# Splitting the first weight panels before a join, and moving modulation panels, in a four-layer hybrid backbone on one core

## The chip, the cores and the metric

One core of a Trainium2 chip runs the whole program. The metric is the device time of one execution in microseconds; the time of a kernel is the median of its runs. The kernel before was run three times: 2142.14 us in the median, 2142.07 to 2143.4 us. TensorE is called PE in the profile, VectorE DVE, ScalarE ACT, GpSimd POOL, and SyncE SP.

## The reference, cut to what matters

```
for i in range(4):                       # mixers: attention, Hyena, S5, FNet
    mod_l = split(silu(c) @ mod_w[i] + mod_b[i], 6)      # the same for ctx with silu(c_ctx)
    hl = modulate(rmsnorm(xl, mix_pre_g[i]), mod_l[0], mod_l[1])
    yl = mixer_i(hl, hc)
    xl = xl + mod_l[2] * rmsnorm(yl, mix_post_g[i])
    hl = modulate(rmsnorm(xl, ffn_pre_g[i]), mod_l[3], mod_l[4])
    xl = xl + mod_l[5] * rmsnorm(swiglu(hl, ffn_w13[i], ffn_w2[i]), ffn_post_g[i])
```

All is float32. There are 256 latent and 256 context tokens, the model is 1024 wide and the SwiGLU 2816. The context is carried through layers 0 and 1 (512 tokens a stage), read by layer 2, and not needed by layer 3, so the later stages work on 256 tokens.

## The kernel before, in words

**Layout.** Activations are held transposed: 8 slices (k or c, 0 to 7) of 128 channels on the partitions, 512 or 256 tokens along the free axis. A float32 product is made of three products of rounded halves: `product` (L930 to L935) multiplies w_hi by h_hi, w_hi by h_lo and w_lo by h_hi. So each weight panel (1024 x 256, 1 MB) goes through `Split` (L840 to L911): it lands in `ring`, which has two slots; ACT rounds it in two halves into w_hi (`round`, L887); DVE subtracts, also in two halves, into w_lo (`remain`, L894). w_hi and w_lo hold two panels each. A slot of the ring is loaded again once its panel is split; SP issues those loads in one fixed order (`sp_issue`, L202).

**Joins.** Between a mixer and its SwiGLU, and between a SwiGLU and the next mixer, stands a `Join` (L530 to L753); there are eight, called here by layer as mid 0, post 0, mid 1, ..., post 3. While the stage before gives its last products, `move` (ACT, L567) and `cross` (DVE, L596) take each slice c: its square, its gain, and the products for the next norm's sum. Then come `root_post` (L643), a reciprocal (L708), five small DVE operations (L713 to L721), `root_pre` (L648) and a second reciprocal (L732). Each of the two results is spread over the partitions by PE (L481), first r_post into bank 5, then r_pre into bank 4. Then, slice by slice, DVE runs scaled (L690), update (L695) and normed (L700), ACT applies the modulation (L673) and rounds (L677), and DVE makes h_lo (L704, `remainder`). Those last two exist where the next stage takes split activations (`parts`): all four mid joins and post 0. There PE starts with `lead_in` (L913): as slice k becomes ready, it does the 12 products of that slice with the first two weight panels; after half of the slices it releases the slot for half of the third panel (`stepped`).

**Panels split around a join.** Where `early` is set (layer 0), the first panel's halves are rounded at c = 5 of `move`; elsewhere ACT rounds them around root_pre. All remainders of the first two panels are on DVE inside `Join.vector`: panel 0 half 0 before scaled(0), then panel 1 half 0 after slice 0, and the other two halves after slices 2 and 3. The first half of panel 2 is rounded after slice 5.

**Modulation panels.** The 24 vectors of mod_l (units) are computed from 96 weight panels of 1 MB, four a unit, each in 8 matmuls of 32 columns that show as 16 rows (L402, bank 7, MODB). `mods.place` gives panels to places in the program in a fixed order; where a place begins after a unit is complete, PE first transposes that unit (`turn`, L377, into bank 6). ACT copies MODB to mod_rows (L413) once the unit's fourth panel is done; DVE reads the transpose in `mods.vector` (L423 to L434). `turn` waits for ACT's copy of its own unit and, by `wait_read`, for DVE's reading of the unit turned before it:

```
def wait_read(self, pe):
    if self.turned_by_pe:
        pe.wait_ge(mod_ready, self.ready0[self.turned_by_pe - 1] + 1)
```

Panels lie in a ring of two (mod_ring). `mods.refill(sp, upto)` (L357) issues the next loads in SP's order, each behind a wait for the use of the panel whose slot it takes.

**Places before.** Layer 0's SwiGLU has 16 panels, behind every other step; mid 0, post 0 and mid 1 have (2, 2): two before the first spread, two behind the second. Post 1 has (2, 0); mid 2, post 2 and mid 3 have (2,). The S5 mixer has 4 ("states"), 2 ("scan") and 2 ("turns").

**The S5 mixer** (L2386 to L2820). PE injects 16 batches of groups and transposes them (L2688, L2707), then multiplies by a Toeplitz matrix (L2725). Meanwhile DVE scans, with POOL for half the groups. ACT copies the states of the first half (`forward`, L2757), and PE multiplies them by the output weights (L2738, first half: 128 matmuls), runs the two "scan" panels, and after ACT's second `forward` the second half. ACT copies the unit of the scan panels before its second forward. DVE reads all modulation units of this mixer only after its scan is finished (`backward`, then `mods.vector`). SP loads, in this order: injection weights, two mod panels, the Toeplitz matrix, output weights of the first half, those of the second half once L2725 is done, mod panels, and, after the scan, the panels of the gated unit (`self.up`, w_glu). In the gated unit ACT makes a sigmoid (L2802), DVE the gated value (L2593), and ACT calls `post.move` (mid 2) one chunk later.

## Time and profile before

| what | value |
|---|---|
| median of three runs | 2142.14 us |
| the profiled execution's own time | 2140.99 us |
| its span | 2139.2 us |
| PE busy (matmul) | 2023.3 us, 95% |
| PE busy (weight load) | 1623.0 us, 76% |
| DVE busy | 1230.4 us, 58% |
| ACT busy | 887.1 us, 41% |
| POOL busy | 166.5 us, 8% |
| DMA | 342.18 MB, mean 160 GB/s |
| granted PE clock, mean | 0.98 |

The busy times are over the whole span; the program is a chain of stages, so an engine that is half idle overall can still be the one that others wait for in a join. The profile's own times start with the span; about 1.8 us of the execution lie around it.

### The profile page before, as it was taken

To read this page: it belongs to the slowest core of one execution; us is meant where nothing else is said; L and a number is where in the kernel's file an instruction comes from. 1 tells how busy PE (TensorE), PEld (TensorE's weight loads), DVE (VectorE), ACT (ScalarE), POOL (GpSimd) and SP (SyncE) were. 2 spreads that over 40 slices of the span, in tenths; PEclk is the share of its full clock that TensorE was granted. 3 is DMA by queue.
4 is the path that set the end of the run, shared out by engine and by line. 5 is a ranking of instruction groups with operands and counts; after the bars stand their busy time and mean duration, and the time that the engine had idled before them with its cause. 6 is when DMAs were issued, how large, how long until landed. Compare 5 with 4: busy or idle time off the path is not lost.

```text
span 2139.2 us, 32361 instructions
## 1 busy us (share of the span) xinstructions
PE 2023.3 (95%) x13489; PEld 1623.0 (76%) x13489; DVE 1230.4 (58%) x2056; ACT 887.1 (41%) x1464; POOL 166.5 (8%) x255
## 2 busy tenths in 40 slices
PE   6999999999999999999999999998658999999998
PEld 4765566777777767767768888876357999789997
DVE  5233553556566557668564665764975645656454
ACT  3432334443333353323553344235645544545444
POOL 0000100102101101001010210020320000000000
PEclk9999999999999999999999999999879999999999
DMA  8434341545435546443243433343984555425552
GB/s 307 160 115 175 132 158 61 166 143 181 173 121 171 195 164 230 158 157 113 94 145 102 133 123 121 121 150 126 334 296 158 178 184 184 157 80 163 185 184 99
DMA packets 227246, 342.18 MB, mean 160 GB/s; under 512 B 9590, under 2 KB 190625, under 8 KB 224860
## 3 DMA queue, kind: packets, MB, share of 16 engines
q1 hardware_dynamic: 216064, 310.27, 42.1%
q0 software_dynamic: 10320, 29.58, 4.7%
q8 instruction: 107, 1.75, 0.3%
q10 hardware_dynamic: 716, 0.26, 0.0%
q14 instruction: 39, 0.32, 0.0%
HBM read 317.66 MB, written 24.51 MB: 160 GB/s over the span
## 4 chain that ended last, share of the span: by engine, by line
PE 85%; DVE 7%; DMA 3%; ACT 2%; POOL 1%; issue 1%; SPq 0%; ACTq 0%; DVEq 0%; POOLq 0%
PE bank L933 24%; PE bank L934 23%; PE bank L935 23%; PE bank L402 3%; PE bank L1417 1%; DMA arena<-mod_w 1%; PE bank L622 1%; PE bank L1848 1%; PE bank L2212 1%; PE bank L612 1%; DMA mod_ring<-mod_w 1%; DMA ring<-s_w_glu 1%; PE bank L2090 1%; PE bank L1391 1%; PE bank L1807 1%
## 5 line engine op out<-in xcount | busy, mean ns | idle before, releaser
L933 PE MATMUL bank<-h_hi,w_hi 128*128 128x512 f32 (+1 forms) x1480 | 511.7, 346 | 11.9 <-DVE h_lo L704 8.1
L934 PE MATMUL bank<-h_lo,w_hi 128*128 128x512 f32 (+1 forms) x1480 | 504.1, 341 | 0.0
L935 PE MATMUL bank<-h_hi,w_lo 128*128 128x512 f32 (+1 forms) x1480 | 504.0, 341 | 0.0
L894 DVE TENSOR_TENSOR w_lo<-ring,w_hi 128x1024 fp32r<-128x1024 f32 (+1 forms) x282 | 323.9, 1185 | 288.1 <-ACT w_hi L887 288.0
L933 PEld LDWEIGHTS bank<-h_hi,w_hi 128*128 128x128 f32 x1480 | 282.6, 191 | 50.4 <-DVE h_lo L704 10.6
L887 ACT ACTIVATE w_hi<-ring 128x1024 fp32r<-128x1024 f32 (+1 forms) x282 | 274.2, 1019 | 104.8 <-PE bank L935 102.5
L935 PEld LDWEIGHTS bank<-h_hi,w_lo 128*128 128x128 f32 x1480 | 282.6, 191 | 32.0 <-issue 0.2
L934 PEld LDWEIGHTS bank<-h_lo,w_hi 128*128 128x128 f32 x1480 | 283.1, 191 | 29.3 <-issue 0.2
L933 PE MATMUL bank<-g_hi,w_hi 128*128 128x512 f32 (+1 forms) x704 | 241.1, 342 | 0.0
L934 PE MATMUL bank<-g_lo,w_hi 128*128 128x512 f32 (+1 forms) x704 | 236.9, 337 | 0.0
L935 PE MATMUL bank<-g_hi,w_lo 128*128 128x512 f32 (+1 forms) x704 | 236.7, 336 | 0.0
L933 PEld LDWEIGHTS bank<-g_hi,w_hi 128*128 128x128 f32 x704 | 133.5, 190 | 22.7 <-issue 8.7
L935 PEld LDWEIGHTS bank<-g_hi,w_lo 128*128 128x128 f32 x704 | 133.6, 190 | 14.2
L934 PEld LDWEIGHTS bank<-g_lo,w_hi 128*128 128x128 f32 x704 | 133.6, 190 | 12.9
L1136 ACT ACTIVATE g_hi<-arena 128x512 fp32r<-128x512 f32 (+1 forms) x88 | 45.9, 525 | 234.5 <-DVE arena L1161 234.5
L1130 ACT ACTIVATE arena<-bank 128x512 f32<-128x512 f32 (+1 forms) x88 | 42.7, 490 | 190.4 <-PE bank L935 188.7
L402 PE MATMUL bank<-mod_ring,silu_c 128*32 128x256 f32 x1408 | 95.4, 394 | 23.1 <-DMA mod_ring<-mod_w 23.1
L1161 DVE TENSOR_TENSOR arena<-arena,bank 128x512 f32<-128x512 f32 (+1 forms) x88 | 48.2, 551 | 111.8 <-PE bank L935 110.5
L402 PEld LDWEIGHTS bank<-mod_ring,silu_c 128*32 128x32 f32 x1408 | 40.4, 111 | 61.5 <-DMA mod_ring<-mod_w 26.7
L933 PE MATMUL bank<-h_hi,hy_w_hi 128*128 128x512 f32 x192 | 76.6, 399 | 0.0
L934 PE MATMUL bank<-h_lo,hy_w_hi 128*128 128x512 f32 x192 | 75.3, 392 | 0.0
L935 PE MATMUL bank<-h_hi,hy_w_lo 128*128 128x512 f32 x192 | 75.0, 391 | 0.0
(391 smaller groups left out, 3179.3 us busy)
## 6 DMA issues: line engine op xcount, KB each, us to landing
ring<-ffn_w SPq DMA_DIRECT2D x120, 1024.0 KB, 5.1
mod_ring<-mod_w SPq DMA_DIRECT2D x88, 1024.0 KB, 6.9
ring<-ffn_w SPq DMA_DIRECT2D x16, 768.0 KB, 4.6
ring<-hy_w_in SPq DMA_DIRECT2D x12, 1024.0 KB, 5.2
arena<-mod_w SPq DMA_DIRECT2D x8, 1024.0 KB, 17.0
s_in_weights<-arena POOLq DMA_DIRECT2D x32, 256.0 KB, 3.0
s_out_weights<-arena POOLq DMA_DIRECT2D x16, 512.0 KB, 3.4
arena<-s_in_weights SPq DMA_DIRECT2D x8, 1024.0 KB, 7.1
```

Of the source, the lines that this page charges most:

```text
L402: last = nc.tensor.matmul(MODB[32 * g:32 * g + 32, 0:256], silu_c[:, k, :], self.slot(m)[:, kk, 256 * g:256 * g + 256], start=(k == 0), st ...
L612: last = nc.tensor.matmul(bank[5][32 * g:32 * g + 32, 0:P], ones[:, :], SQ[:, c, g * P:(g + 1) * P], start=(c == 0), stop=(c == KD - 1))
L622: last = nc.tensor.matmul(bank[4][32 * g:32 * g + 32, 0:2 * P], ones[:, :], self.zx[:, c % 2, g, :, :].rearrange("p z t -> p (z t)"), star ...
L887: nc.scalar.activation(self.hi[:, i % SPLIT, a:b], self.w.slot(i)[:, a:b], ACT.Copy).then_inc(w_rounded, 1)
L894: last = unit.tensor_tensor(self.lo[:, i % SPLIT, c:c + w], self.w.slot(i)[:, c:c + w], self.hi[:, i % SPLIT, c:c + w].bitcast(F32), ALU.s ...
L933: nc.tensor.matmul(o, w[0], v[0], start=first, stop=False)
L934: nc.tensor.matmul(o, w[0], v[1], start=False, stop=False)
L935: return nc.tensor.matmul(o, w[1], v[0], start=False, stop=last)
L1130: nc.scalar.activation(self.silus[:, q, 0:n], self.out(i, q)[:, 0:n], ACT.Silu).then_inc(ffn_silu, 1)
L1136: nc.scalar.activation(g_hi[:, c + q, 0:n], self.silus[:, q, 0:n], ACT.Copy).then_inc(ffn_g_rounded, 1)
L1161: nc.vector.tensor_tensor(self.silus[:, q, 0:n], self.silus[:, q, 0:n], self.out(i, q)[:, 0:n], ALU.mult).then_inc(ffn_product, 1)
L1391: nc.tensor.matmul(b[:, :], self.qn[:, hd, q], self.kn[:, hd, :], start=True, stop=False)
```

## The change

The first two weight panels behind each join with `first` are rounded inside `move` (c = 4, 5, 6; all four halves at c = 4 for mid 2). For the mid joins DVE makes their remainders inside `cross` (c = 5 and 6; for mid 2 in the S5 mixer's loop at c = 5); post 0 keeps DVE's old order. The third panel's first half is rounded behind all slices. The first spread comes before the modulation panels, and each spread is followed by one panel (post 2, mid 2 and mid 3 had two before the first). The four panels so freed in layer 0 and two of mid 1's go elsewhere: layer 0's SwiGLU takes 20 instead of 16, and the S5 mixer 10 instead of 8: two ("turned") behind the injections, two ("states") and two ("late") behind the Toeplitz product, then "scan" and "turns" as before. Refills stand in front of the output weights of each half. Buffers of the S5 and FNet mixers are moved out of the way of w_hi and w_lo.

```diff
@@ class Join
+            ROUNDS = {4: ((0, 0), (0, 1)), 5: ((1, 0),), 6: ((1, 1),)}
+            REMAINDERS = {5: ((0, 0), (1, 0)), 6: ((0, 1), (1, 1))}
...
@@ Join.move
-                if self.early and c == KD - 3:
-                    self.first.round(act, 0, 0)
-                    self.first.round(act, 0, 1)
+                if self.first:
+                    for panel, half in self.rounds.get(c, ()):
+                        self.first.round(act, panel, half)
@@ Join.cross
+                if self.first:
+                    for panel, half in self.remainders.get(c, ()):
+                        self.first.remain(dve, panel, half)
@@ Join.tensor
+                pe.wait_ge(*self.small.after(1))
+                spread(bank[5], r_post, self.n).then_inc(j_spread, 1)
                 if self.fills:
                     mods.tensor(pe, (self, 0))
-                pe.wait_ge(*self.small.after(1))
-                spread(bank[5], r_post, self.n).then_inc(j_spread, 1)
@@ Join.scalar
-                if self.first and not self.early:
-                    self.first.round(act, 0, 0)
                 self.root_pre(act)
-                if self.first:
-                    if not self.early:
-                        self.first.round(act, 0, 1)
-                    self.first.round(act, 1, 0)
-                    if self.parts:
-                        self.first.round(act, 1, 1)
...
-                        if k == 5:
-                            self.first.round(act, 2, 0)
+                if self.first:
+                    self.first.round(act, 2, 0)
@@ Join.vector
-                if self.first:
+                if self.first and not self.remainders:
                     self.first.remain(dve, 0, 0)
...
-                        if k == 0:
-                            self.first.remain(dve, 1, 0)
-                        if k in (2, 3):
-                            self.first.remain(dve, k - 2, 1)
+                        if not self.remainders:
+                            if k == 0:
+                                self.first.remain(dve, 1, 0)
+                            if k in (2, 3):
+                                self.first.remain(dve, k - 2, 1)
@@ class S5
+            ROUNDS = {4: ((0, 0), (0, 1), (1, 0), (1, 1))}
+            REMAINDERS = {"gates": 5}
...
-                mods.place((self, "states"), 4, p0 + 0.4)
+                mods.place((self, "turned"), 2, p0 + 0.3)
+                mods.place((self, "states"), 2, p0 + 0.35)
+                mods.place((self, "late"), 2, p0 + 0.4)
                 mods.place((self, "scan"), 2, p0 + 0.4)
@@ S5.sync
                 for c in range(8):
                     toeplitz(c)
+                mods.refill(sp, p0 + 0.3)
                 sp.wait_ge(self.e_summed, self.injected(self.NB - 1))
                 for hf in range(2):
                     if hf:
                         sp.wait_ge(self.m_summed, 1)
+                        mods.refill(sp, p0 + 0.35)
@@ S5.vector
                 self.backward(dve, V.tensor_copy, 1, self.moved_dve)
-                for key in ("states", "scan"):
+                for key in ("turned", "states", "late", "scan"):
                     mods.vector(dve, (self, key))
...
+                    if c == self.REMAINDERS["gates"]:
+                        for half in range(2):
+                            for panel in range(2):
+                                self.post.first.remain(dve, panel, half)
@@ S5.tensor
+                mods.tensor(pe, (self, "turned"))
                 pe.wait_ge(self.m_loaded, 16 * (1 + 8))
...
-                mods.tensor(pe, (self, "states"))
+                for key in ("states", "late"):
+                    mods.tensor(pe, (self, key))
@@ S5.scalar
-                mods.scalar(act, (self, "states"))
+                for key in ("turned", "states", "late"):
+                    mods.scalar(act, (self, key))
@@ stages
-        TICKS = {0: lambda i: i % 2 if i < 32 else 0, 1: lambda i: 0, 2: lambda i: 0, 3: lambda i: 0}
+        TICKS = {0: lambda i: int(i % 3 > 0 and i < 30), 1: lambda i: 0, 2: lambda i: 0, 3: lambda i: 0}
...
             if l < 2:
-                mid.place_mods()
+                mid.place_mods((1, 1))
             else:
-                mid.place_mods((2,))
+                mid.place_mods((1, 1))
             ffn = Ffn(l, n_out, mid, post, TICKS[l])
             if l == 0:
-                post.place_mods()
+                post.place_mods((1, 1))
             if l == 1:
-                post.place_mods((2, 0), (len(panels) + 0.2, None))
+                post.place_mods((1, 1), (len(panels) + 0.2,) * 2)
             if l == 2:
-                post.place_mods((2,))
+                post.place_mods((1, 1))
```

## Rows read from the trace of the kernel before

**Rows 1.** The page's groups: ACT's rounding of half a panel (busy, mean ns | idle)

```profile
L887 ACT ACTIVATE w_hi<-ring 128x1024 fp32r<-128x1024 f32 (+1 forms) x282 | 274.2, 1019 | 104.8 <-PE bank L935 102.5
```

**Rows 2.** Timeline of mid 0: start, duration, engine, line, operation, [idle before <- releaser]

```profile
362.37 1.91 PE L402 MATMUL bank<-mod_ring,silu_c 128*32 128x256 f32 x32
...
364.06 1.22 DVE L894 TENSOR_TENSOR w_lo<-ring,w_hi 128x1024 fp32r<-128x1024 f32 x1
...
365.40 0.69 DVE L690 TENSOR_TENSOR arena<-arena,bank 128x512 f32<-128x512 f32 x1
...
370.78 0.69 DVE L704 TENSOR_TENSOR h_lo<-arena,h_hi 128x512 fp32r<-128x512 f32 x1
...
371.22 1.07 PE L402 MATMUL bank<-mod_ring,silu_c 128*32 128x256 f32 x16 [1.41 <-DMA mod_ring<-mod_w]
...
384.53 0.50 PE L933 MATMUL bank<-h_hi,w_hi 128*128 128x512 f32 x1 [0.52 <-DVE h_lo L704]
...
395.55 0.38 PE L377 MATMUL bank<-ident,mod_rows 128*128 128x128 f32 x2
```

**Rows 3.** Timeline of mid 1

```profile
1087.10 0.69 DVE L690 TENSOR_TENSOR arena<-arena,bank 128x512 f32<-128x512 f32 x1 [0.52 <-PE bank L481]
...
1092.47 0.69 DVE L704 TENSOR_TENSOR h_lo<-arena,h_hi 128x512 fp32r<-128x512 f32 x1
...
1117.46 0.38 PE L377 MATMUL bank<-ident,mod_rows 128*128 128x128 f32 x2
```

**Rows 4.** Timeline of post 0

```profile
804.77 0.69 DVE L704 TENSOR_TENSOR h_lo<-arena,h_hi 128x512 fp32r<-128x512 f32 x1
...
816.71 0.38 PE L377 MATMUL bank<-ident,mod_rows 128*128 128x128 f32 x2
```

**Rows 5.** Timeline of PE in mid 2 and mid 3 (256 tokens)

```profile
1656.06 0.48 PE L933 MATMUL bank<-h_hi,w_hi 128*128 128x256 f32 x1 [2.11 <-DVE h_lo L704]
...
1671.75 0.38 PE L377 MATMUL bank<-ident,mod_rows 128*128 128x128 f32 x2
...
1927.66 0.58 PE L933 MATMUL bank<-h_hi,w_hi 128*128 128x256 f32 x1 [2.11 <-DVE h_lo L704]
...
1940.35 0.39 PE L933 MATMUL bank<-h_hi,w_hi 128*128 128x256 f32 x1 [0.81 <-DVE h_lo L704]
...
1943.33 0.38 PE L377 MATMUL bank<-ident,mod_rows 128*128 128x128 f32 x2
```

**Rows 6.** Timeline of DVE in post 1 and post 2: the first use of bank 5

```profile
1490.35 0.69 DVE L690 TENSOR_TENSOR arena<-arena,bank 128x512 f32<-128x512 f32 x1 [1.26 <-PE bank L481]
...
1861.93 0.42 DVE L690 TENSOR_TENSOR arena<-arena,bank 128x256 f32<-128x256 f32 x1 [0.82 <-PE bank L481]
```

**Rows 7.** The chain in order of time: a modulation panel, a weight panel's load

```profile
395.93 1.00 PE bank L402 x16
...
1660.97 5.21 DMA ring<-ffn_w
```

**Rows 8.** End of the S5 mixer: SP's loads and ACT's sigmoid

```profile
1628.50 8.47 SPq L213 DMA_DIRECT2D ring<-ffn_w  x2
...
1641.03 0.47 ACT L2802 ACTIVATE arena<-bank,vec 128x256 f32<-128x256 f32 x1 [6.68 <-PE bank L935]
```

**Rows 9.** Timeline of the S5 mixer around the end of the scan

```profile
1563.27 1.94 PE L402 MATMUL bank<-mod_ring,silu_c 128*32 128x256 f32 x16 [15.24 <-DMA mod_ring<-mod_w]
...
1570.31 5.37 PE L2738 MATMUL bank<-arena,tail 128*32 128x128 f32 x128 [2.70 <-ACT tail L2757]
...
1576.73 0.17 DVE L423 TENSOR_TENSOR modv<-bank,vec 128x16 f32<-128x16 f32 x1
...
1577.92 2.82 SPq L213 DMA_DIRECT2D ring<-s_w_glu  x2
```

**Rows 10.** Windows in that mixer: length, busy of five engines, PEclk, DMA share, GB/s

```profile
1555.00:1560.00 5.00, 0.00 (x0) 0.00 (x0) 4.69 (x13) 0.00 (x0) 4.84 (x3) 0.50 1.00 414
```

**Rows 11.** DMA issues from 1540 to 1550 us: times, KB, median us to landing

```profile
mod_ring<-mod_w SPq DMA_DIRECT2D x2, 1024.0 KB, 17.0
```

More of the change, by code:

```diff
@@ L530, in build, with __init__ @@
         class Join:
-            def __init__(self, n, post, pre, scratch, parts=False, split=False, early=False):
+            ROUNDS = {4: ((0, 0), (0, 1)), 5: ((1, 0),), 6: ((1, 1),)}
+            REMAINDERS = {5: ((0, 0), (1, 0)), 6: ((0, 1), (1, 1))}
+            def __init__(self, n, post, pre, scratch, parts=False, split=False, rounds=ROUNDS, remainders=REMAINDERS):
                 self.n, self.post, self.pre, self.zx = n, post, pre, scratch
-                self.parts, self.split, self.early = parts, split, early
+                self.parts, self.split = parts, split
+                self.rounds, self.remainders = rounds, remainders
                 self.rows = n // 4
@@ L2461, in __init__ @@
                 p0 = len(panels)
-                mods.place((self, "states"), 4, p0 + 0.4)
+                mods.place((self, "turned"), 2, p0 + 0.3)
+                mods.place((self, "states"), 2, p0 + 0.35)
+                mods.place((self, "late"), 2, p0 + 0.4)
                 mods.place((self, "scan"), 2, p0 + 0.4)
                 mods.place((self, "turns"), 2, p0 + RING)
-                self.y_hi, self.y_lo = (place(n, KD * TOK + a, [KD, LAT], F32R) for n, a in (("s5_y_hi", 10240), ("s5_y_lo", 8192)))
+                self.y_hi, self.y_lo = (place(n, KD * TOK + a, [KD, LAT], F32R) for n, a in (("s5_y_hi", 24576), ("s5_y_lo", 26624)))
                 self.y_rounded, self.y_split = Tally(mix_rounded, KD), Tally(mix_split, KD)
-                hi, lo = (place(n, KD * TOK + 12288 + i * SPLIT * KD * 256, [SPLIT, KD * 256], F32R) for i, n in enumerate(("s5_w_hi", "s5_w_lo")))
+                slots = place("s5_w", KD * TOK + 16384, [SPLIT, 2, KD * 256], F32R)
+                hi, lo = slots[:, :, 0], slots[:, :, 1]
                 self.up = Gated("s5_glu", A["s5_w_glu"][0], D, lambda k: (self.y_hi[:, k, :], self.y_lo[:, k, :]), LAT,
@@ L2824, in __init__ @@
                 self.f_hi = place("fn_f_hi", KD * TOK + 26624, [KD, LAT], F32R)
-                self.f_lo = place("fn_f_lo", KD * TOK + 13568, [KD, LAT], F32R)
+                self.f_lo = place("fn_f_lo", 3 * P * KD * 8 + KD * TOK, [KD, LAT], F32R)
                 hi, lo = (place(n, KD * TOK + 16384 + i * SPLIT * KD * 256, [SPLIT, KD * 256], F32R) for i, n in enumerate(("fn_w_hi", "fn_w_lo")))
@@ L2913, in build @@
                 joins.append(Opening(stages[0], mod))
-            joins.append(Join(spans[l][1], (mod, 1), (mod, 2), scratch["arena" if l == 0 else "tail"], parts=True, early=(l == 0)))
+            joins.append(Join(spans[l][1], (mod, 1), (mod, 2), scratch["arena" if l == 0 else "tail"], parts=True,
+                              rounds=S5.ROUNDS if l == 2 else Join.ROUNDS, remainders=S5.REMAINDERS if l == 2 else Join.REMAINDERS))
             nxt = [m for m in live if m > l]
             pre = (Modulation(nxt[0]), 0) if nxt else None
-            joins.append(Join(spans[l][1], (mod, 3), pre, scratch["tail"], parts=(l == 0), split=(l == 1), early=(l == 0)))
+            joins.append(Join(spans[l][1], (mod, 3), pre, scratch["tail"], parts=(l == 0), split=(l == 1), remainders={}))
         stages.append(joins[0])
```

## The prediction

> **What bounds the kernel.** I read the page first. PE is busy for 95% of the span (the table above), so a step of PE that is moved costs time unless it falls into one of PE's gaps. The chain of waits, in order of time, shows where those gaps are: at the joins, at the end of the S5 mixer's scan, and at some loads. So I went through each join and through that mixer in the timeline, engine by engine.
>
> In mid 0 the reader should see three things. Two modulation panels hold PE for 1.91 us, from 362.37, in front of the first spread. Bank 5 is first used at 365.40. Slice 0 of h_lo is complete at 371.47, but PE still waits for a modulation load (371.22) and does that panel before it starts the lead-in. From slice 4 on (384.53) the lead-in runs without a wait to 395.55: 11.02 us for 4 slices, 2.755 a slice [rows 2].
>
> **Lead-ins of 512 tokens.** The change takes four remainders of 1.2 us [rows 2] out of DVE's sequence in the mid joins and puts the spread in front of the panels. In mid 0 the small operations end when the first remainder begins, at about 364.1 (the durations of neighbours overlap a little); scaled(0) starts at 364.15 instead of at 365.40, and the second reciprocal, the second spread and slice 0 follow 1.25 us earlier: h_lo(0) at 370.2. DVE then has four operations of at most 0.69 us a slice, no more than PE's 2.755, so PE runs through: 370.25 + 8 x 2.755 = 392.3 instead of 395.55 [rows 2]. **Mid 0: -3.25.** The rounding moved into `move` lies beside the mixer's last products: PE takes 2 x 2.755 us for an output slice, and ACT rounds half a panel in 1.02 us [rows 1], at most two a slice. Were that cover gone, four halves would cost 4.1. Of the panels behind the spreads, one each is loaded before the join, so none waits there.
>
> Mid 1 has the same shape. There scaled(0) waited 0.52 for the spread behind a remainder; without both it starts at 1085.45 instead of 1087.10, so h_lo(0) ends at 1093.16 - 1.65 = 1091.5, and the lead-in at 1113.55 instead of 1117.46 [rows 3]. **-3.9.**
>
> Post 0 keeps DVE's order. Only PE's panels get out of the way, and slice 4, complete at 805.46, still sets the end: 805.46 + 11.02 = 816.5 against 816.71 [rows 4]. **-0.2**, though two panels fewer stand there.
>
> **Lead-ins of 256 tokens.** Mid 3 starts at 1927.66 and ends at 1943.33; its last two slices take 2.98 us [rows 5] with a slow first product, so 1.45 a slice. The remainder taken out in front of scaled(0) brings 0.9 (the root then ends last, not the remainder). End: 1926.76 + 8 x 1.45 = 1938.35. **Mid 3: -5.0.** Mid 2 starts at 1656.06 and ends at 1671.75 [rows 5]; in the same way 1655.16 + 11.6 = 1666.75, **-5.0**. The third panel's load, which used to wait for the split of the first, starts before its need in both.
>
> Mid 2 pays for it in front. All four roundings stand behind slice 4 there. SwiGLU panel 1 is issued last of the two loads, at 1628.50 + 8.47 - 0.37 = 1636.6 [rows 8]; a free load takes 5.2 [rows 7], so it lands at 1641.8. ACT stands behind that wait in its order, then has two roundings of 1.02 [rows 1]: until 1643.9. The sigmoid of chunk 6, which started at 1641.03 [rows 8], is queued behind it; DVE's three remaining remainders run until 1646.3, 4.8 us after it used to take chunk 6. About 1.6 us of idle time between that and `move` absorb a part. **+3.2**, between 2.8 and 4.8.
>
> **Joins without early panels.** In post 1 and post 2 DVE waited 1.26 and 0.82 us for bank 5, behind the panels [rows 6]. The first becomes **-1.25**; of the second the root leaves **-0.7**.
>
> **Layer 0's SwiGLU** gets four more panels. Each costs PE its 1.00 us [rows 7], as PE has no gap there: **+4.0**.
>
> **The S5 mixer** is where the change has a wait of its own. Before, unit 19 was transposed and read in layer 1's SwiGLU, so `turn` of unit 20 had nothing to wait for at the "states" panels. Now the shifted count completes unit 19 in post 1; it is transposed in "turned", and DVE reads it only after the scan, at 1576.73 [rows 9]. The "late" place begins with `turn(20)`, whose `wait_read` asks for just that reading. PE stands there, and behind it stand the late panels and the first half's output product, which started at 1570.31. From DVE's 1576.9: transpose 0.4, two late panels 2 x 1.9 (at the duration of 1563.27), output product 5.4, two scan panels 1.9 [rows 9, 2], and 0.5 for SP: 1588.9. Their use lets SP go on to the gated unit's weights, issued at 1577.92 before: +11.0. ACT's second `forward` hangs on the scan panels too. The scan panels' own loads are issued behind the late panels at 1579.3 and 1581.1; with 5.2 each [rows 7] they land by 1586.5, as the output product ends.
>
> How fast PE is there is open. Around the scan's end PE idles, and its granted clock is 0.50 of full speed, the 1.2 GHz level [rows 10]; one panel took 1.94 us there against 0.95 in the joins [rows 9, 2]. At full clock throughout, late panels cost 1.9 and the product perhaps half of 5.4, and only the loads (1584.8 for the second) hold the rest: +8.9. I take **+10.5**, nearer to the slow end, as those rows stand in the same place after the same idling.
>
> The Trainium skill ("TensorE: Matmul & The Clock Gate", section "What's actually happening") says that an idle array is throttled by default and only activity releases it. By that rule alone the late panels would be slow and the sum 0.5 us higher; the rows agree at 0.50 with PE idle. It speaks against the change: the refilled gap lies behind the longest idling.
>
> The "turned" and "states" panels lie in PE's wait for the Toeplitz load and behind that product; without the hold they would be hidden. The two loads that go in front of each half's output weights delay these by some 5 us each, long before their use.
>
> **Sum.** -3.25 - 3.9 - 0.2 - 5.0 - 5.0 + 3.2 - 1.25 - 0.7 + 4.0 + 10.5 = -1.6. Against the profiled execution's 2140.99 that is 2139.4; the median lies 1.15 above that execution, so 2140.5. A measurement of this kernel can tell about 0.2% (4.3 us) from no change.
>
> **Rivals.** (a) *PE isn't held in the S5 mixer*: if DVE's reading comes earlier than I read the order, the late panels hide as before, and 10.5 goes: 2130.0. For it: before, PE idled 15.24 us there at no cost [rows 9]. Against it: one semaphore, one order of DVE's program. 12%.
>
> (b) *Slower*: the loads behind the hold are late. The scan panels' loads can only start once the late panels are used, and the gated unit's weights follow them in SP's order. In this mixer mod loads took 17.0 us to land when output weights stood in front of them [rows 11]. At that, the second lands at 1598.1, the scan panels end at 1599.1, and SP follows at 1599.6: +21.7 instead of +10.5, 2151.7. It decides from a landing of about 6 us on; it makes the whole kernel measurably slower from about 12. Against it: the output weights, issued at some 1550, are gone when the hold ends, and the queue is empty. 8%.
>
> (c) *The lead-ins still stop*: DVE's and ACT's operations, or the third panel's load, pace them rather than PE. Two stops of 0.5 us, like those of 0.52 and 0.81 now [rows 2, 5], in each of the four mid lead-ins make 4.0: 2144.5. For it: DVE's four operations are as long as PE's share of a slice. Against it: the durations overlap, and the 1.2-us remainders were what broke the pace. 12%.
>
> **Numbers.** The forecast has 68%; its own bounds (+8.9 to +11.5 for the hold, 2.8 to 4.8 in mid 2, half a microsecond for each join) give 2137 to 2144. Rival (a) lies below, (c) at the upper edge. The range 2133 to 2146 leaves out (a)'s centre, (b) and little else. Faster by over 0.2% needs 2137.9 or less: (a) with 12%, and 14% from the forecast's lower edge, 26%. Slower by over 0.2% needs 2146.4: (b), and a little of (c), 10%. The rest, 64%, is no change.
>
> **What would show it.** Each mid join's lead-in without a wait for h_lo, 22.0 us long at 512 and 11.6 at 256 tokens; bank 5's first use without a wait for PE; ACT waiting for a ring load behind slice 4 in the S5 mixer's end. Above all PE's L377 in the S5 mixer released by DVE's L423, 30 us after the states panels, the output product some 11 us after ACT's first forward, and the next load of w_glu that much later. The prediction falls if L402 ("late") is released by its load around 1560 and the output product follows ACT directly, or if the lead-ins still stop at slices 3 and 4.

## The result and the profile after

The changed kernel takes 2147.51 us (median of 14 runs, 2146.01 to 2148.59) against 2142.16 (14 runs of the kernel before beside it): a ratio of 1.0024, 95% interval 1.0016 to 1.0031. It is slower by 5.4 us, where 2140.5 was forecast with a range up to 2146. The profiled execution took 2146.01 us with a span of 2144.2, 5.0 more than the span before.

The page's head, after: PE is busy for as long as before (2022.7 us against 2023.3), so the 5 us are waiting, not work.

```profile
span 2144.2 us, 32362 instructions
PE 2022.7 (94%) x13489; PEld 1617.9 (75%) x13489; DVE 1230.0 (57%) x2056; ACT 887.9 (41%) x1464; POOL 166.5 (8%) x255
PEclk9999999999999999999999999999879999999998
```

Where they arise is read best from one instruction that stands at the same place of every join: ACT's root of the output norm (L643 before, L652 after, two or three lines lower in some experiments). The table has its first start and then the time from each join's root to the next one's, all from the timeline of ACT. The experiments of the next section are in it too. Each row is one profiled execution, which lies up to 3.5 us from the median of its kernel (e8), so medians and rows need not differ by the same amount.

| kernel | mid 0 at | to post 0 | to mid 1 | to post 1 | to mid 2 | to post 2 | to mid 3 | to post 3 | span |
|---|---|---|---|---|---|---|---|---|---|
| before | 360.97 | 421.00 | 300.15 | 403.80 | 162.00 | 210.26 | 61.36 | 207.70 | 2139.2 |
| after | 360.43 | 421.92 | 300.81 | 400.83 | 176.66 | 207.73 | 60.66 | 202.72 | 2144.2 |
| e1 | 361.50 | 423.56 | 301.08 | 399.48 | 164.09 | 206.61 | 62.26 | 202.74 | 2133.3 |
| e2 | 361.02 | 421.97 | 299.96 | 401.07 | 177.89 | 207.74 | 60.67 | 202.75 | 2145.5 |
| e3 | 361.90 | 423.50 | 299.72 | 401.05 | 169.36 | 211.03 | 60.67 | 204.21 | 2143.4 |
| e4 | 361.33 | 421.23 | 301.69 | 405.46 | 163.92 | 207.20 | 60.99 | 203.28 | 2137.1 |
| e5 | 360.69 | 421.93 | 300.50 | 401.06 | 161.80 | 206.91 | 60.67 | 203.28 | 2128.8 |
| e6 | 360.79 | 421.94 | 300.26 | 401.04 | 164.47 | 207.29 | 60.85 | 202.74 | 2131.3 |
| e7 | 361.18 | 421.38 | 298.66 | 401.14 | 173.89 | 207.35 | 60.77 | 202.75 | 2139.1 |
| e8 | 360.80 | 419.96 | 298.88 | 401.33 | 167.54 | 207.41 | 60.71 | 202.73 | 2131.3 |
| e9 | 360.65 | 421.93 | 300.59 | 401.08 | 162.09 | 206.74 | 62.28 | 203.99 | 2131.3 |
| e10 | 360.48 | 421.93 | 300.60 | 400.98 | 161.35 | 211.08 | 62.28 | 205.37 | 2136.0 |
| e11 | 360.65 | 425.23 | 300.55 | 402.73 | 162.61 | 207.32 | 60.86 | 202.74 | 2134.6 |

One column stands out: the stretch with post 1 and the S5 mixer became 14.66 us longer. All others together became 10.1 us shorter up to the last root (the earlier start of mid 0, 0.5, is in this), and 0.5 was lost behind it.

**The S5 mixer.** PE's timeline of the changed kernel around the scan (start, duration, engine, line, operation, idle time before it and releaser); it answers to [rows 9]:

```profile
1529.22 0.38 PE L377 MATMUL bank<-ident,mod_rows 128*128 128x128 f32 x2
...
1537.41 6.22 PE L2740 MATMUL bank<-arena 128*32 128x128 f32 x128 [5.94 <-DMA arena<-s_toeplitz]
1543.45 1.90 PE L402 MATMUL bank<-mod_ring,silu_c 128*32 128x256 f32 x32
1573.30 0.66 PE L377 MATMUL bank<-ident,mod_rows 128*128 128x128 f32 x2 [27.95 <-DVE modv L423]
1573.88 3.32 PE L402 MATMUL bank<-mod_ring,silu_c 128*32 128x256 f32 x32
1577.03 3.67 PE L2754 MATMUL bank<-arena,tail 128*32 128x128 f32 x128
1580.99 1.07 PE L402 MATMUL bank<-mod_ring,silu_c 128*32 128x256 f32 x16 [0.29 <-DMA mod_ring<-mod_w]
1584.97 1.07 PE L402 MATMUL bank<-mod_ring,silu_c 128*32 128x256 f32 x16 [2.91 <-DMA mod_ring<-mod_w]
```

Unit 19 is transposed at 1529.22 and read by DVE at 1572.97; `turn(20)` in front of the late panels waits 27.95 us for that reading, as forecast. The first output product stands behind it. ACT's `forward` and `backward` (L2773) ran from 1562.38 for 4.03 us, so the product could have started at about 1566.5; it started at 1577.03. Then comes a second wait, of 2.91 us, for the load of the second scan panel. SP's own timeline gives the end of the chain, again against [rows 9]:

```profile
1575.88 10.59 SPq L363 DMA_DIRECT2D mod_ring<-mod_w  x4
1586.57 1.04 SPq L213 DMA_DIRECT2D ring<-s_w_glu  x2
```

The gated unit's weights are issued at 1586.57 instead of 1577.92. DVE's reading came 3.76 us earlier than before (1572.97 against 1576.73), so from that reading on the loss is 8.65 + 3.76 = 12.4 us.

**The joins.** PE in mid 0 and post 0, after, against [rows 2] and [rows 4]:

```profile
365.11 1.16 PE L481 MATMUL bank<-r_pre,sel 128*128 128x128 f32 x8 [1.02 <-DVE r_pre L733]
366.20 1.07 PE L402 MATMUL bank<-mod_ring,silu_c 128*32 128x256 f32 x16
369.63 0.50 PE L935 MATMUL bank<-h_hi,w_hi 128*128 128x512 f32 x1 [2.35 <-DVE h_lo L705]
...
391.61 1.07 PE L402 MATMUL bank<-mod_ring,silu_c 128*32 128x256 f32 x16
...
788.17 2.01 PE L481 MATMUL bank<-r_pre,sel 128*128 128x128 f32 x8 [2.15 <-DVE r_pre L733]
790.12 1.81 PE L402 MATMUL bank<-mod_ring,silu_c 128*32 128x256 f32 x16
793.54 0.50 PE L935 MATMUL bank<-h_hi,hy_w_hi 128*128 128x512 f32 x1 [1.61 <-DVE h_lo L705]
```

In mid 0 the lead-in runs from 369.63 to 391.61 without a stop, 21.98 us for the 22.04 forecast. In post 0 the spread takes 2.01 instead of 1.16 us: PE has idled for 2.15 us behind its single panel and works more slowly. The same in mid 2, where PE comes out of the mixer's end, with the windows of that stretch (length; busy PE, PEld, DVE, ACT, POOL; PEclk; DMA share; GB/s):

```profile
1662.38 1.22 PE L481 MATMUL bank<-r_post,sel 64*128 64x128 f32 x4
1663.53 1.93 PE L402 MATMUL bank<-mod_ring,silu_c 128*32 128x256 f32 x16
1665.45 1.22 PE L481 MATMUL bank<-r_pre,sel 64*128 64x128 f32 x4
1666.59 1.93 PE L402 MATMUL bank<-mod_ring,silu_c 128*32 128x256 f32 x16
1668.78 0.58 PE L935 MATMUL bank<-h_hi,w_hi 128*128 128x256 f32 x1 [0.25 <-DVE h_lo L705]
```

```profile
1656.00:1660.00 4.00, 1.82 (x14) 0.67 (x16) 2.34 (x10) 3.11 (x7) 0.00 (x0) 0.83 0.00 0
1660.00:1664.00 4.00, 3.23 (x20) 1.51 (x24) 2.74 (x8) 0.98 (x3) 0.00 (x0) 0.50 0.00 0
...
1668.00:1672.00 4.00, 3.75 (x23) 3.22 (x16) 3.82 (x13) 3.08 (x7) 0.00 (x0) 0.50 1.01 354
1672.00:1676.00 4.00, 4.00 (x34) 4.00 (x34) 3.97 (x13) 3.06 (x7) 0.00 (x0) 0.96 1.04 370
```

PE's clock stands at its lower level, 0.50, from the first spread to the first 3 us of the lead-in. Mid 3 of the same execution has the same code and the same 256 tokens, and there PE is at full speed; its lead-in starts 7.22 us behind the root (8.13 in mid 2) and ends 18.83 us behind it (21.28):

```profile
1930.43 0.71 PE L481 MATMUL bank<-r_post,sel 64*128 64x128 f32 x4
1933.43 0.71 PE L481 MATMUL bank<-r_pre,sel 64*128 64x128 f32 x4 [1.29 <-DVE r_pre L733]
...
1936.26 0.39 PE L935 MATMUL bank<-h_hi,w_hi 128*128 128x256 f32 x1 [1.11 <-DVE h_lo L705]
```

### The profile page after: what moved, and what is told of

The parts are those of the page before. It is cut to its first block, busy times and chain, and to the rows that moved or that the text cites. A ratio compares the mean times of both kernels' runs of the same rounds, so it can differ in the third digit from the quotient of the medians.

```text
span 2144.2 us, 32362 instructions
## 1 busy us (share of the span) xinstructions
PE 2022.7 (94%) x13489; PEld 1617.9 (75%) x13489; DVE 1230.0 (57%) x2056; ACT 887.9 (41%) x1464; POOL 166.5 (8%) x255
## 4 chain that ended last, share of the span: by engine, by line
PE 86%; DVE 7%; DMA 2%; ACT 2%; POOL 1%; issue 1%; SPq 1%; ACTq 0%; DVEq 0%; POOLq 0%
PE bank L935 24%; PE bank L936 23%; PE bank L937 23%; PE bank L402 3%; PE bank L1419 1%; PE bank L1850 1%; PE bank L2214 1%; PE bank L631 1%; DMA ring<-mla_w_in 1%; DMA mod_ring<-mod_w 1%; PE bank L621 1%; PE bank L2092 1%; DVE arena L701 1%; PE bank L1393 1%; PE bank L1809 1%
```

## Experiments

Theory H: DVE's late reading of unit 19 holds PE, and that is the S5 mixer's loss. Rival R1: the two extra loads and the refills in front of the output weights. Rival R2: the moved splits bring nothing. For the mid 2 join there were three more theories: B, that ACT's wait for a load costs time (e5); C, that the late load of the third panel does (e6); K, that PE comes to the join slow and the panels there don't matter (e10). Edits are against the changed kernel unless said.

### e1: DVE reads unit 19 between the halves of the scan

```diff
                 for hf in range(2):
+                    if hf:
+                        mods.vector(dve, (self, "turned"))
                     for gs in self.PARTS[hf]:
...
-                for key in ("turned", "states", "late", "scan"):
+                for key in ("states", "late", "scan"):
                     mods.vector(dve, (self, key))
```

> The changed kernel with one step moved: DVE reads unit 19 (mods.vector of "turned") between the two halves of the scan, at about 1535, instead of behind the scan at 1572.97. Theory H (the late read holds PE): L377 of the "late" place starts right behind the "states" panels, at about 1545, the late panels are done before 1556, the first output product follows ACT's forward at about 1566, and the gated unit's first weights are issued 12.4 us earlier than in the changed kernel (about 1574 instead of 1586.57): 2147.5 - 12.4 = 2135. Rival R1 (the two extra loads and refills in front of the output weights are what delays the mixer): those stay as they are, so the time stays within 1.5 us of 2147.5.

Measured: 2135.06 us (2133.66 to 2137.69), ratio to the kernel before 0.9966 (0.9953 to 0.9979). Its PE timeline:

```profile
1546.09 0.44 PE L377 MATMUL bank<-ident,mod_rows 128*128 128x128 f32 x2 [0.47 <-ACT mod_rows L413]
...
1558.69 1.93 PE L402 MATMUL bank<-mod_ring,silu_c 128*32 128x256 f32 x16 [0.50 <-DMA mod_ring<-mod_w]
1568.09 5.73 PE L2756 MATMUL bank<-arena,tail 128*32 128x128 f32 x128 [7.47 <-ACT tail L2775]
1573.64 1.91 PE L402 MATMUL bank<-mod_ring,silu_c 128*32 128x256 f32 x32
1578.13 5.37 PE L2756 MATMUL bank<-arena,tail 128*32 128x128 f32 x128 [2.57 <-issue]
```

`turn` goes through at 1546.09, the late panels are done by 1560.6 and the output product waits for ACT alone. SP issues the gated unit's weights at 1576.08 instead of 1586.57 (1574 was expected). The stretch to mid 2 is 164.09 instead of 176.66: the hold costs 12.6 us. One reading moved in DVE's program turns a change that loses 5 us into one that wins 7. Theory H stands.

### e2: the refills behind all output weights, the late reading kept

```diff
-                mods.place((self, "turned"), 2, p0 + 0.3)
-                mods.place((self, "states"), 2, p0 + 0.35)
+                mods.place((self, "turned"), 2, p0 + 0.4)
+                mods.place((self, "states"), 2, p0 + 0.4)
```

> The changed kernel with both refills in the S5 mixer put behind all eight output-weight loads, and DVE's late read kept. Theory H: the loads then land after 1550 but long before the hold ends at 1573.3, so PE's L377 still is released by DVE's L423 at 1573 and the time stays at 2147.5 within 1.5. Rival R1 (refills in front of the output weights delay the mixer): some 10 us go, 2137.

Measured: 2148.51 us (2144.93 to 2150.53), ratio 1.0025 (1.0016 to 1.0035), level with the changed kernel. The panels come later and the hold ends at the same time:

```profile
1559.95 1.94 PE L402 MATMUL bank<-mod_ring,silu_c 128*32 128x256 f32 x16 [17.43 <-DMA mod_ring<-mod_w]
...
1573.20 0.66 PE L377 MATMUL bank<-ident,mod_rows 128*128 128x128 f32 x2 [8.90 <-DVE modv L423]
```

R1 falls: with the refills out of the way the mixer isn't faster (177.89 against 176.66), and e1 gained its 12.6 us with the two extra loads and the refills in their place.

### e3: no panels between the output products

```diff
-                mods.place((self, "scan"), 2, p0 + 0.4)
+                mods.place((self, "scan"), 0, p0 + 0.4)
...
-        TICKS = {..., 2: lambda i: 0, 3: lambda i: 0}
+        TICKS = {..., 2: lambda i: int(i in (4, 6)), 3: lambda i: 0}
```

> The changed kernel without the two panels behind the first output product (they go to SwiGLU 2, at 1.0 us each, so +2.0). The hold by DVE's late read stays. Theory H with the load as a term of its own: PE's second output product no longer waits for a panel's load (2.91) and its panel (1.07 twice), and starts about 6 us earlier, and SP issues the gated unit's weights at the late panels' use (about 1577 instead of 1586.57): 2147.5 - 7 + 2 = 2142.5, between 2140 and 2144. If instead the length of the hold alone counts (DVE's read at 1573), and the scan panels lie beside ACT's second forward, 2147.5 - 1 + 2 = 2148.5.

Measured: 2144.28 us (2143.33 to 2147.82), ratio 1.0010 (1.0000 to 1.0019). The hold is there (L377 released by DVE's L423 after 27.91 us), but SP issues the gated unit's weights 4.90 us behind DVE's reading instead of 13.60 (1586.57 - 1572.97):

```profile
1575.40 0.17 DVE L423 TENSOR_TENSOR modv<-bank,vec 128x16 f32<-128x16 f32 x1
...
1580.30 3.11 SPq L213 DMA_DIRECT2D ring<-s_w_glu  x2
```

The mixer's stretch is 7.3 us shorter, as expected; the total is just outside the 2140 to 2144. So the load that may only start when the held panels are used, and the panels that wait for it, make up to 7.3 us behind a hold. How much the same panels would cost without the hold was not run, so this is an upper bound for their share of the 12.6. The whole kernel gains 3.2, for the two panels cost SwiGLU 2 3.3 us (211.03 against 207.73) instead of 2.0, and the last stretch has 1.5 more.

### e4: the code of the change with the panels placed as before

S5 mixer 8 panels without "turned", SwiGLU 0 16, mid 0, post 0 and mid 1 two behind each spread.

```diff
-                mods.place((self, "turned"), 2, p0 + 0.3)
-                mods.place((self, "states"), 2, p0 + 0.35)
+                mods.place((self, "turned"), 0, p0 + 0.4)
+                mods.place((self, "states"), 2, p0 + 0.4)
...
-        TICKS = {0: lambda i: int(i % 3 > 0 and i < 30), ...
+        TICKS = {0: lambda i: i % 2 if i < 32 else 0, ...
...
-                mid.place_mods((1, 1))
+                mid.place_mods((2, 2))
...
-                post.place_mods((1, 1))
+                post.place_mods((2, 2))
```

> The code of the changed kernel with the placement of the kernel before in mid 0, post 0, mid 1 (2 + 2 panels), SwiGLU 0 (16) and the S5 mixer (8, no "turned" panels, all refills behind the output weights): the early splits and the order of spread and panels alone. Theory H: no hold (-12.4), SwiGLU 0 -4.0, and the lead-ins of mid 0, post 0 and mid 1 give back up to 3 us each, as two panels stand behind each spread and the second of a pair waits for its load: 2147.5 - 12.4 - 4.0 + 4 = 2135, between 2131 and 2140, and faster than the kernel before (2142.2). Rival R1 expects it too. Rival R2 (the moved splits themselves bring nothing or cost): 2142 or above, level with the kernel before.

Measured: 2139.80 us (2137.77 to 2141.59), ratio 0.9985 (0.9976 to 0.9995): faster than before, at the upper end of what was expected. PE in mid 0:

```profile
366.01 1.16 PE L481 MATMUL bank<-r_pre,sel 128*128 128x128 f32 x8 [0.15 <-DVE r_pre L733]
370.26 1.84 PE L402 MATMUL bank<-mod_ring,silu_c 128*32 128x256 f32 x16 [3.09 <-DMA mod_ring<-mod_w]
372.74 1.58 PE L402 MATMUL bank<-mod_ring,silu_c 128*32 128x256 f32 x16 [0.63 <-DMA mod_ring<-mod_w]
374.25 0.50 PE L935 MATMUL bank<-h_hi,w_hi 128*128 128x512 f32 x1
```

The modulation ring has two slots, so the second pair's loads start only when the first pair is used, and PE waits 3.09 us for them with slice 0 of h_lo ready. The lead-in starts at 374.25 instead of 369.63. Having only one panel behind each spread is thus worth the four more panels in SwiGLU 0 (4.0 us): without it mid 0, post 0 and mid 1 lose 3.3, 0.9 and 4.6 us (the table's columns, SwiGLU 0 counted at 4.0). The mixer has no hold here either, and its stretch is 163.92, level with e1's 164.09: two different edits that free PE give the same length.

### e5: e1, with mid 2's second panel split behind later slices

```diff
-            ROUNDS = {4: ((0, 0), (0, 1), (1, 0), (1, 1))}
-            REMAINDERS = {"gates": 5}
+            ROUNDS = {4: ((0, 0), (0, 1)), 5: ((1, 0),), 6: ((1, 1),)}
+            REMAINDERS = {"gates": {5: ((0, 0), (0, 1)), 6: ((1, 0),), 7: ((1, 1),)}}
...
-                    if c == self.REMAINDERS["gates"]:
-                        for half in range(2):
-                            for panel in range(2):
-                                self.post.first.remain(dve, panel, half)
+                    for panel, half in self.REMAINDERS["gates"].get(c, ()):
+                        self.post.first.remain(dve, panel, half)
```

> The kernel with the early read (e1, 2135.06), and in the S5 mixer's end the second SwiGLU panel rounded behind slices 5 and 6 and its remainders behind gates 6 and 7, instead of all of it behind slice 4. Theory B (ACT standing 5.9 us for the load of panel 1, with the sigmoids queued behind it, is what mid 2's early split costs, 3.3 us): the wait shrinks to 2 us or less, the roundings then cost up to 2: 1 to 2 us are won, 2133.5. Rival (the four roundings and remainders themselves cost it, 4 x 1.02 on ACT and 4 x 1.2 on DVE, wherever they stand): level with e1, 2135.

Measured: 2132.25 us (2130.60 to 2135.61), ratio 0.9950 (0.9938 to 0.9963). ACT in the changed kernel, and then in e5:

```profile
1643.49 1.99 ACT L889 ACTIVATE w_hi<-ring 128x1024 fp32r<-128x1024 f32 x2
1651.21 2.01 ACT L889 ACTIVATE w_hi<-ring 128x1024 fp32r<-128x1024 f32 x2 [5.72 <-DMA ring<-ffn_w]
```

```profile
1631.25 1.99 ACT L889 ACTIVATE w_hi<-ring 128x1024 fp32r<-128x1024 f32 x2
1638.02 0.47 ACT L2819 ACTIVATE arena<-bank,vec 128x256 f32<-128x256 f32 x1 [4.78 <-PE bank L937]
...
1639.61 1.04 ACT L889 ACTIVATE w_hi<-ring 128x1024 fp32r<-128x1024 f32 x1
```

The sigmoid is no longer queued behind a load: in e5 it goes first and the rounding finds its panel there. The stretch to mid 2 is 161.80 against e1's 164.09. The other kernels without the hold and without the two further panels of e7 agree: 161.4 to 162.6 with this edit (e9, e10, e11), 164.5 without it (e6). Theory B stands, with 2.3 us.

### e6: e1, with mid 2's refills behind the load of SwiGLU 2's third panel

```diff
-                mid.place_mods((1, 1))
+                mid.place_mods((1, 1), (len(panels) + (3 if l == 2 else 2),) * 2)
```

> The kernel with the early read (e1, 2135.06), with the two refills of mid 2 issued behind the load of SwiGLU 2's third panel and not in front of it. Theory C (in mid 2 SP stands at the refill until PE has used the panel behind the second spread, and the third panel's load behind it lands 2.12 us after ACT asks for it, so that PE waits for its remainder at the end of the lead-in): the load is issued up to 10 us earlier, ACT and DVE take the panel without a wait, PE goes on right behind the lead-in: 1.0 to 1.5 us are won, 2133.8. Rival (DVE's eight slices end last anyway): level with e1.

Measured: 2133.35 us (2133.05 to 2134.86), ratio 0.9955 (0.9942 to 0.9968). ACT takes the third panel in e1 behind a wait, in e6 without:

```profile
1667.92 1.06 ACT L889 ACTIVATE w_hi<-ring 128x1024 fp32r<-128x1024 f32 x1 [2.12 <-DMA ring<-ffn_w]
```

```profile
1665.01 1.04 ACT L889 ACTIVATE w_hi<-ring 128x1024 fp32r<-128x1024 f32 x1
```

The wait is gone, and yet the stretch from mid 2 to post 2 takes 207.29 against e1's 206.61. The 96 products of the lead-in show why the two can't be compared: in e6 11 of them took over 0.35 us, in e1 one. Where the clock was nearly alike, in e5 (7 of them) and e9 (5), the same edit brings 0.17 (206.91 and 206.74), and the two slow products fewer explain that. What e6's total gains over e1 stands in stretches that the edit doesn't touch (mid 0: 421.94 against 423.56, post 2: 60.85 against 62.26; see the section on the hardware). Theory C falls with its 1.0 to 1.5: the late load was real, and no gain from removing it can be told from the clock.

### e7: two more panels in the mixer

On e1; DVE reads unit 19 in front of `across`, and SwiGLU 0 has 18 panels.

```diff
                 mods.place((self, "late"), 2, p0 + 0.4)
+                mods.place((self, "more"), 2, p0 + 0.4)
...
-        TICKS = {0: lambda i: int(i % 3 > 0 and i < 30), ...
+        TICKS = {0: lambda i: int(i % 3 > 0 and i < 27), ...
```

> The kernel with the early read, with two more panels ("more") behind the "late" ones in the S5 mixer and 18 in SwiGLU 0 instead of 20; DVE reads unit 19 in front of the second half's across. Theory H: PE still waits for ACT's forward there, so the pair is hidden but for some tenths (their loads can only start at about 1558 and land at 1565, PE takes them until about 1568, where the output product started in e1): -2.0 + 0.5, 2133.5. Rival (the pair's loads delay the output product and with it the gated unit's weights): level with e1 or slower, 2135 to 2137.

Measured: 2139.71 us (2137.68 to 2142.45), ratio 0.9986 (0.9977 to 0.9995), 4.6 more than e1.

```profile
1567.63 1.94 PE L402 MATMUL bank<-mod_ring,silu_c 128*32 128x256 f32 x16 [9.24 <-DMA mod_ring<-mod_w]
...
1571.64 3.67 PE L2757 MATMUL bank<-arena,tail 128*32 128x128 f32 x128
...
1580.55 1.93 PE L402 MATMUL bank<-mod_ring,silu_c 128*32 128x256 f32 x16 [4.37 <-DMA mod_ring<-mod_w]
```

The expectation took a load that lands 7 us after its issue. It took 12.8 us (issued at 1554.83, used at 1567.63), because the output weights (issued from 1544.50 on, 16.2 us to landing in the median) were still in the DMA queue, which moved 414 to 428 GB/s with a busy share of 1.0 from 1540 to 1565. ACT's `forward` and `backward` ran from 1560.66 for 4.03 us, so the output product could have started at 1564.7; it started at 1571.64, and the scan panels' loads behind it were late in turn (4.37). The mixer's stretch is 9.8 us longer than e1's. The rival stands, and the loss is larger than the 2135 to 2137 that it allowed.

### e8: e5, e6 and e7 together

> The edits of e5, e6 and e7 together. If each brings what its theory says (1.5, 1.2, 1.5) and they don't overlap: 2131, between 2129.5 and 2133, faster than both kernels (ratio to the kernel before about 0.9945). If two of the three fall: 2133.5 or above.

Measured: 2136.62 us (2133.10 to 2140.31), ratio 0.9970 (0.9959 to 0.9981). The two more panels take back more than e5 brought in the mixer: 167.54 in the mixer's stretch against e5's 161.80. So the pair costs 5.7 us here and 9.8 in e7; in e7 PE waited 4.37 us for the second scan panel, here 1.44.

### e9: e5 and e6 together

> The early read (e1), the roundings and remainders of mid 2 spread over slices (e5) and its refills behind the third panel's load (e6), without the two more panels. The two later edits act at different places: 2135.06 - 2.8 - 1.7 = 2130.6, between 2129.5 and 2132, ratio to the kernel before about 0.9945. If they overlap (with e5 the lead-in's end no longer waits for the load): 2132.2, as e5.

Measured: 2133.08 us (2130.60 to 2137.82), ratio 0.9955 (0.9941 to 0.9968): not told apart from e5 alone, which agrees with e6's edit bringing nothing; the 2130.6 that was expected isn't reached. e5 and e9 beat both kernels, by about 10 us and 15 us.

### e10: e9 without panels in mid 2

```diff
-                mid.place_mods((1, 1), (len(panels) + (3 if l == 2 else 2),) * 2)
+                mid.place_mods((1, 1) if l == 3 else (0, 0), (len(panels) + (3 if l == 2 else 2),) * 2)
...
-        TICKS = {..., 2: lambda i: 0, 3: lambda i: 0}
+        TICKS = {..., 2: lambda i: int(i in (4, 6)), 3: lambda i: 0}
```

> As e9, with no modulation panel in mid 2 (both go to SwiGLU 2 at 1.0 us each). Theory K (in mid 2 PE comes cold from waiting, and what it does there it does at half speed: the panel behind the second spread ends with h_lo's slice 0): the lead-in starts at most 0.3 us earlier, its first products are slow for some 3 us as before, +2.0 for the panels moved and -0.3: 2132.3. Rival (the two panels of 1.93 us are what holds the lead-in up): it starts 1 to 2 us earlier, 2131. Other way round (the panels wake PE, and without them more of the lead-in is slow): 2133 to 2134.

Measured: 2138.16 us (2136.08 to 2140.23), ratio 0.9975 (0.9966 to 0.9984), 5.1 more than e9. The lead-in does not start earlier: 8.12 us behind the root of mid 2 in both (1645.34 to 1653.46; in e9 1646.34 to 1654.46), now with 2.11 us of waiting for h_lo.

```profile
1653.46 0.58 PE L935 MATMUL bank<-h_hi,w_hi 128*128 128x256 f32 x1 [2.11 <-DVE h_lo L705]
```

The windows of e10:

```profile
1652.00:1656.00 4.00, 2.54 (x12) 2.54 (x13) 3.82 (x13) 3.07 (x7) 0.00 (x0) 0.50 0.01 2
1656.00:1660.00 4.00, 4.00 (x25) 4.00 (x25) 4.00 (x14) 3.06 (x7) 0.00 (x0) 0.65 0.01 4
```

Its windows show the clock at 0.50 until beyond 1656, while e9's has 1.00 from 1656 on, with 36 products instead of 25 in the same 4 us. So DVE's chain sets the start, not the panels, and with the panels PE is back at full speed sooner (5 of the 96 products over 0.35 us in e9, 24 in e10): the third of the three expectations, in its direction. Its 2133 to 2134 was too low. The stretch from mid 2 to post 2 is 4.34 us longer than e9's: the lead-in with its slow products makes 1.6 of it, which leaves 2.7 for the two panels in SwiGLU 2 instead of 2.0. Another 1.4 stands in mid 3 (205.37 against 203.99), where the code is the same.

### e11: e9 without the early splits of mid 0 and mid 1

```diff
-                              rounds=S5.ROUNDS if l == 2 else Join.ROUNDS, remainders=...
+                              rounds=S5.ROUNDS if l == 2 else Join.ROUNDS if l == 3 else {5: ((0, 0), (0, 1))},
+                              remainders=S5.REMAINDERS if l == 2 else Join.REMAINDERS if l == 3 else {}))
```

and panel 1 rounded behind `root_pre`, as before.

> As e9, with the early splits of mid 0 and mid 1 undone: the roundings of panel 1 behind root_pre, one remainder in front of scaled(0), the others behind slices 0, 2 and 3; spread order and panel counts stay as they are. By the working of the prediction (1.25 us for scaled(0) and slice 0, and stops of 0.3 to 0.8 behind the remainders): +1.5 to +2.5 in each of the two joins, 2130.6 + 4 = 2134.6. Rival (the new order of spread and panels alone brought the gain of 3.25 and 3): level with e9.

Measured: 2139.36 us (2134.22 to 2142.11), ratio 0.9980 (0.9971 to 0.9989). Mid 0's stretch is 3.3 us longer than e9's (425.23 against 421.93), mid 1's 1.65 (402.73 against 401.08): 4.95 for the 4 expected; the medians differ by 6.3. In mid 0 the lead-in starts at 370.98 and ends at 395.13, 24.15 us instead of 21.98. How the 4.95 divides between the two joins isn't shown: 8 products of e11's lead-in in mid 0 took 0.6 us, where e9 has none, and in mid 1 it is the other way round (none in e11, 7 in e9). By e1 against the changed kernel, 8 such products lengthen a lead-in by about 1.6 us, so the two shifts roughly cancel in the sum. The early splits bring most of what the joins of 512 tokens gained; R2 falls for them. For mid 2 and mid 3 no run takes the early splits out while keeping the new order of spread and panels, so their share there is not shown.

## Why the prediction was wrong

The waits and their order were right. PE was held by L423 as described, the late panels and the output product behind it, and the lead-ins of 512 tokens ran through. What failed are sizes: six terms of the sum, five of them in the same direction, above all mid 2 (2.5 us), the hold (2.1) and post 0 and mid 1 (0.9 each). The "from" column says where a value was read; "table" is the table of the joins above.

| step | predicted | measured | from |
|---|---|---|---|
| mid 0 and SwiGLU 0 | -3.25 + 4.0 | +0.9 | table |
| post 0 | -0.2 | +0.7 | table |
| mid 1 | -3.9 | -3.0 | table |
| post 1 | -1.25 | -1.9 | root to ACT's first shift: 6.66, before 8.59 |
| the hold in the S5 mixer | +10.5 | +12.6 | e1 |
| ACT behind panel 1's load | +3.2 | +4.0 | rest of the mixer's stretch (14.66 + 1.9 - 12.6) |
| mid 2 | -5.0 | -2.5 | table |
| post 2 | -0.7 | -0.7 | table |
| mid 3 | -5.0 | -5.0 | table |
| start of mid 0, end | 0 | -0.5, +0.5 | table |
| sum | -1.6 | +5.0 | |

**The hold** failed on "with 5.2 each they land by 1586.5, as the output product ends". The two loads of 1 MB were issued at 1575.88 and 1577.28 and moved together: the first was used 5.1 us later, at 1580.99, the second 7.7 us later, at 1584.97. The product itself ended early, 3.67 us long at the risen clock instead of 5.4, so that PE waited 2.91. The slow end was right for the late panels (3.32 for two, at 0.50), the fast end for the product. The lower bound, +8.9 for a PE at full speed, rested on the same 5.2; by its own figures (1584.8 for the load, 1.0 for the panel, 0.5 for SP) it is +8.4. Rival (b), loads behind the hold that decide from a landing of about 6 us on, was the right mechanism: with 7.7 instead of its 17.0 us PE waited 0.29 and 2.91, and the hold came out 2.1 above the term where (b) had 11.2.

The Trainium skill ("TensorE: Matmul & The Clock Gate", "What's actually happening") has it that throttling is the default state and activity releases it. The rows agree on both sides of the hold: 0.50 while PE waited, and a product at full speed behind two slow panels. The prediction drew from it only that the late panels would be slow, and not that they would warm the product.

**Mid 2** failed twice, on one cause, the clock. "The remainder taken out brings 0.9": the lead-in starts 8.13 us behind the root (1660.65 to 1668.78), as before (1647.92 to 1656.06), because both spreads, which lie in DVE's chain, took 1.22 us instead of the 0.71 of before. "8 x 1.45 = 11.6": it lasts until L377 at 1681.93, 13.15 us, the first three microseconds at half speed (0.41 a product against 0.28). Before, the windows show full speed up to 1656 and 0.57 in the 4 us behind it: the slow start of the lead-in was there already, and the prediction's 1.45 a slice, read from the last two slices of mid 3, left it out. Mid 3 of the changed kernel shows both terms as they were forecast, with PE at full speed: 7.22 us from the root to the lead-in, 0.9 less than before, and 11.61 us for the lead-in. It is 2.45 us shorter than mid 2 from root to L377, which is the missing 2.5.

Why PE is slow in mid 2 stays open. ACT's wait of 5.72 us isn't needed for it: e5 has no such wait, and both its spreads take 1.22 too, as does the first one in every kernel with the new order. In e1 the second took 0.71, the lead-in started 7.61 us behind the root, and the stretch was 1.1 us shorter. What the new order takes away is two panels that PE did in front of the first spread; that these kept it at full speed is not tested.

**Post 0 and mid 1** assumed full speed too. In post 0 PE idles 2.15 us between its single panel and the second spread, which then took 2.01 us. The kernels with this code differ just there: in e3 the same spread takes 1.16, L377 follows the root after 34.37 us and the stretch is 299.72; in the changed kernel L377 follows after 35.21 and the stretch is 300.81. The term (34.5 by its own figures) held for a PE at full speed. In mid 1 the lead-in had 6 products of 0.63 us or more and its stretch was 400.83. In e1, with the same code there, it had none, and the stretch was 399.48, which is 4.3 less than before where 3.9 was forecast. In e2, e3, e5, e6, e9 and e10 7 or 8 products were slow, and the stretch was 401.0 to 401.1.

**ACT in mid 2** (+4.0) lay in the stated bounds; e5 shows that 2.3 of it is the wait. **Post 1** gained more than the 1.25 us that DVE had waited for bank 5: the second spread came 1.35 us earlier behind the root (4.68 instead of 6.03) and took 1.16 us instead of 1.74. **Mid 0, post 2, mid 3 and SwiGLU 0** came out within 0.2.

None of these was large. Together they made 6.6 us, 2.1 in the hold and 4.3 in joins whose terms assumed PE at full speed. They lifted the result over the range, whose bounds took the slow clock for the hold and left it out for the joins. A change forecast as 1.6 us faster, and most likely no change that can be measured, came out 0.24% slower; the prediction had given that side 10%.

## What to carry to other kernels

When work is moved into an idle stretch of one engine, look for the reader of the result moved with it: a wait for "has been read" ties the idle engine to another one's program order, and a read placed a few lines earlier was worth 12.6 us here. Work in a gap needs its load in the gap too: a two-slot ring makes each pair wait for the use of the pair before, and behind other transfers a load landed in 12.8 us instead of 5.2. And a join from which work of PE is taken need not be shorter by that work: where PE came back slow, the small spreads that everyone waits for took 1.22 us instead of 0.71 and 2.01 instead of 1.16.

## What the hardware showed

The clock made runs of the same code differ. In the stretch between post 2 and mid 3 e5 and e9 are the same instructions, and PE waited 2.19 us for the same operation in front of the same 16 products:

```profile
1865.88 3.72 PE L2867 MATMUL bank<-arena,h_sb 128*128 128x256 f32 x16 [2.19 <-DVE arena L2886]
```

```profile
1866.08 5.41 PE L2867 MATMUL bank<-arena,h_sb 128*128 128x256 f32 x16 [2.19 <-DVE arena L2886]
```

3.72 us in e5 and 5.41 in e9, and the stretches 60.67 and 62.28. In mid 0's stretch six kernels with the same code there show 421.9 to 422.0 and two (e1, e3) 423.5; all eight wait 2.35 us in front of the lead-in, and then 8 of e1's products and 7 of e3's took about 0.63 us instead of 0.40, and none of the others'. So the same short wait of PE may or may not cost 1.6 us more, and nothing in the rows of the stage tells what decides it. The Trainium skill ("TensorE: Matmul & The Clock Gate", "What's actually happening") says that how many products are slow differs from run to run of one kernel; the rows here show it between kernels at the same place. A term below about 1.5 us can't be read from one profile's total, only from its own rows.

Loads that share the queue: a 1 MB panel landed after 5.2 us with little in the queue [rows 7], after 7.7 when another had been issued 1.4 us before it, and after 12.8 behind the output weights, at a queue that moved up to 428 GB/s.
